# Transposes of a normalised x, a new order in the mixer's units, and GpSimd additions ahead of the products with ones

## The reference, cut to what matters

```python
y = xf * lax.rsqrt(jnp.mean(xf * xf, axis=-1, keepdims=True) + EPS)      # of x, then times g
...
s = jnp.einsum('bclhd,bcmhd->bchlm', q, k) * jnp.exp(log_d - m_row[..., None])
num = jnp.einsum('bchlm,bcmhe->bclhe', s, v) + ...
den = jnp.sum(s, axis=-1) + ...
h = num / jnp.maximum(jnp.abs(den), jnp.exp(-m_row))
...
xs = jax.vmap(lambda ub, ib: ub[ib])(u, idx)                             # the rows of each expert
```

## Time and profile before

| | us |
|---|---|
| median of 3 runs | 2302.24 |
| lowest and highest | 2298.16, 2304.51 |
| profiled execution, its time | 2301.57 |
| its span in the trace | 2299.4 |
| TensorE busy | 2134.0 (93%) |
| VectorE busy | 716.3 (31%) |
| ScalarE busy | 647.1 (28%) |
| GpSimd busy | 33.2 (1%) |
| DMA, mean rate | 315 GB/s |

### The profile page before, as it was taken

How to read it: one execution, slowest core, us unless ns; L and a number is a source line. 1 busy time by engine, 2 the same in 40 slices (tenths; PEclk the granted TensorE clock), 3 DMA queues, 4 the chain that set the end, 5 groups by cost and what they waited for, 6 DMA issues and landing times.

```text
span 2299.4 us, 27379 instructions
## 1 busy us (share of the span) xinstructions
PE 2134.0 (93%) x12059; PEld 1317.9 (57%) x12059; DVE 716.3 (31%) x1033; ACT 647.1 (28%) x1022; POOL 33.2 (1%) x54
## 2 busy tenths in 40 slices
PE   8999999889888988988988988989999999989999
PEld 8877444324323333333432432337888998978997
DVE  7756200100110010010010010016665554865653
ACT  6545200101001001001000010005465444865442
POOL 2100000000000000000000000000000000000000
PEclk9999999999999999999999999999999999999999
DMA  7435999999999999999999999997444655544653
GB/s 226 141 90 217 415 424 422 424 424 421 425 424 421 425 425 421 425 425 421 424 425 421 423 424 419 425 422 231 132 147 147 203 190 197 179 148 130 198 191 113
DMA packets 179807, 724.66 MB, mean 315 GB/s; under 512 B 11598, under 2 KB 109314, under 8 KB 130538
## 3 DMA queue, kind: packets, MB, share of 16 engines
q1 hardware_dynamic: 178472, 720.86, 79.4%
q0 software_dynamic: 640, 1.43, 0.2%
q10 hardware_dynamic: 578, 0.64, 0.1%
HBM read 721.82 MB, written 1.07 MB: 314 GB/s over the span
## 4 chain that ended last, share of the span: by engine, by line
PE 62%; DMA 30%; ACT 4%; DVE 3%; issue 1%; DVEq 0%; SPq 0%; ACTq 0%
PE bank L1250 21%; DMA weight_ring<-in_w_up_dram 17%; PE bank L1208 13%; DMA weight_ring<-in_w_gate_dram 12%; PE bank L1134 7%; PE bank L1109 5%; PE bank L777 3%; PE bank L1080 2%; PE bank L1279 1%; PE bank L1186 1%; PE bank L972 1%; PE bank L895 1%; ACT weights_ring L1981 1%; ACT squares L1916 1%; PE bank L1444 1%
## 5 line engine op out<-in xcount | busy, mean ns | idle before, releaser
L1134 PE MATMUL bank<-weight_ring,arena 128*64 128x506 f32 x3048 | 657.4, 573 | 130.3 <-DMA weight_ring<-in_w_up_dram 86.5
L1134 PEld LDWEIGHTS bank<-weight_ring,arena 128*64 128x64 f32 x3048 | 219.3, 137 | 570.1 <-issue 322.8
L1208 PE MATMUL bank<-weight_ring,arena 128*64 128x512 f32 x1408 | 305.7, 593 | 0.0
L2664 DVE TENSOR_TENSOR weights_ring<-weight_ring,weights_ring 128x2048 fp32r<-128x2048 f32 x110 | 249.6, 2289 | 147.5 <-ACT weights_ring L1981 147.3
L2632 DVE SCALAR_TENSOR_TENSOR arena<-arena,bank 128x506 f32<-128x506 f32 (+1 forms) x48 | 28.0, 638 | 822.5 <-ACT arena L1884 822.5
L1250 PE MATMUL bank<-input_high,weights_ring 128*128 128x256 f32 x1920 | 248.1, 281 | 0.0
L1250 PEld LDWEIGHTS bank<-input_high,weights_ring 128*128 128x128 f32 x1920 | 234.3, 188 | 2.7 <-issue 2.5
L1981 ACT ACTIVATE weights_ring<-weight_ring 128x2048 fp32r<-128x2048 f32 x110 | 207.4, 1908 | 62.1 <-DMA weight_ring<-in_w_ffn_down_dram 41.0
L1208 PEld LDWEIGHTS bank<-weight_ring,arena 128*64 128x64 f32 x1408 | 99.2, 137 | 195.0 <-issue 194.9
L1878 ACT ACTIVATE arena<-bank 128x512 f32<-128x512 f32 x16 | 9.6, 597 | 512.0 <-PE bank L1109 512.0
L1250 PE MATMUL bank<-input_low,weights_ring 128*128 128x256 f32 x960 | 132.1, 279 | 0.0
(11 more groups left out here) (388 smaller groups left out, 2003.9 us busy)
## 6 DMA issues: line engine op xcount, KB each, us to landing
weight_ring<-in_w_gate_dram SPq DMA_DIRECT2D x128, 1408.0 KB, 16.2
weight_ring<-in_w_down_dram SPq DMA_DIRECT2D x127, 1408.0 KB, 24.4
weight_ring<-in_w_up_dram SPq DMA_DIRECT2D x126, 1408.0 KB, 24.1
weight_ring<-in_w_ffn_gu_dram SPq DMA_DIRECT2D x44, 1024.0 KB, 5.1
weight_ring<-in_w_ffn_down_dram SPq DMA_DIRECT2D x22, 1024.0 KB, 4.8
weight_ring<-in_w_in_dram SPq DMA_DIRECT2D x16, 1024.0 KB, 5.7
arena<-in_w_xkv_dram SPq DMA_DIRECT2D x8, 2048.0 KB, 25.2
weight_ring<-in_ab_w_in_dram SPq DMA_DIRECT2D x12, 1024.0 KB, 6.1
```

The lines of the kernel that those rows point to most:

```text
L1134: last = pe.matmul(bank[first_bank + c][MPAD * half:MPAD * half + MPAD, 0:(hi - lo) * HF], xs3[:, s, :], w[:, lo:hi, HF * half:HF * half + ...
L1208: last = pe.matmul(bank[6][MPAD * half:MPAD * half + MPAD, :], hidT[:, at:at + MPAD], W[:, j * D + 512 * half:j * D + 512 * half + 512], s ...
L2664: dve.tensor_tensor(low_slot(k), raw_slot(k), high_slot(k), ALU.subtract).then_inc(S("weights_low"), 1)
```

## The change

- Start: ScalarE squares tiles 0 and 2, VectorE tile 1. The diagonal goes; VectorE scales each tile of x by its rate into `xnorm` (over the same space of the decay tables), and TensorE transposes it against the identity. TensorE's order is: tile 0, the first two of tile 1, the small vectors, the first two of tile 2, then the other six pairs.
- Units: GpSimd adds, after the probabilities of unit n, the parts of the key tiles that overlap into `key_sum` (two additions), and TensorE's products with ones run over that sum and what is left: two products over 128 and 144 columns in a forward unit, three over 128, 144 and 128 in a backward one. The values' product goes first; the ones wait for GpSimd. The semaphore `decay_ready` becomes `pool_mixer` and counts on.
- VectorE's product of unit n - 1 moves ahead of the arguments of unit n + 1; ScalarE's `hm_rates` moves ahead of the take of the projection.
- The retention scores of head 1: the wait for the last unit's product moves from the first of three products to the third.
- Token sums: VectorE adds square 7 too, and one group of sums is left, behind the router's products.
- First gather: copy, transposes and copy run in two halves (banks 7 and 5); TensorE waits for the second half ahead of weight slot 2.

```diff
@@ -197,8 +197,7 @@
 vrow = QKP[:, 0:256]
-x_squares = DEC[:, 0:D]
-rate_diag = tiles(DEC[:, D:D + TT * P], TT)
+xnorm = tiles(DEC[:, 0:TT * D], TT)
 mix_high_a = rounded("mixer_high_a", "weight_ring", CSLOTS * CSLOT, 7 * T)
@@ -465,6 +464,12 @@
 STREAM_BANKS = [4, 0, 1, 2]
+key_sum = rows[0]
+def unit_sum_ready(n):
+    return H * TT + 2 * n + 2
 MLSTM_C = 0.25 * float(P) ** -0.5
@@ -506,7 +511,7 @@
         if k == 15:
-            sp.wait_ge(S("decay_ready"), H * TT)
+            sp.wait_ge(S("pool_mixer"), H * TT)
             sp.wait_ge(S("rot_out"), 2 * H)
@@ -688,7 +693,20 @@
         blk = dec[0:ROWS[i], h, i, P * i:P * i + ROWS[i]]
-        pool.tensor_tensor(blk, blk, ident[0:ROWS[i], 0:ROWS[i]], ALU.add).then_inc(S("decay_ready"), 1)
+        pool.tensor_tensor(blk, blk, ident[0:ROWS[i], 0:ROWS[i]], ALU.add).then_inc(S("pool_mixer"), 1)
+    for n in range(8):
+        pt = tiles(SQ[:, (n % 2) * 816:(n % 2 + 1) * 816], TT)
+        lo, hi = (P, T) if n % 2 == 0 else (0, P)
+        pool.wait_ge(S("m_probs"), n + 1)
+        if n:
+            pool.wait_ge(S("num_ready"), n)
+        pool.tensor_tensor(key_sum[:, lo:hi], pt[:, 0, lo:hi], pt[:, 1, lo:hi], ALU.add).then_inc(S("pool_mixer"), 1)
+        pool.wait_ge(S("pool_mixer"), unit_sum_ready(n) - 1)
+        if n % 2 == 0:
+            lo = 2 * P
+        part = key_sum[0:ROWS[2], lo:hi]
+        pool.tensor_tensor(part, part, pt[0:ROWS[2], 2, lo:hi], ALU.add).then_inc(S("pool_mixer"), 1)
@@ -721,22 +739,27 @@
     pe.wait_ge(S("ident_landed"), 16)
-    xt3 = tiles(xtok, TT)
...
-        return pe.matmul(bank[i][:, P * j:P * j + ROWS[j]], xt3[0:ROWS[j], j, P * i:P * i + P],
-                         rate_diag[0:ROWS[j], j, 0:ROWS[j]], start=True, stop=True)
-    pe.wait_ge(S("x_rate"), 1)
+        return pe.transpose(bank[i][:, P * j:P * j + ROWS[j]], xnorm[0:ROWS[j], j, P * i:P * i + P],
+                            ident[0:ROWS[j], 0:ROWS[j]])
+    pe.wait_ge(S("ident_landed"), 16)
+    pe.wait_ge(S("x_steps"), 2)
     for i in range(KT):
         turn_x(i, 0)
+    pe.wait_ge(S("x_steps"), 3)
+    turn_x(0, 1)
+    turn_x(1, 1)
     pe.wait_ge(S("vec_landed"), 16 * sum(len(g) for g in VEC_ROWS))
...
     last.then_inc(S("vec_ready"), 1)
-    pe.wait_ge(S("x_rate"), 3)
-    for i in range(KT):
+    pe.wait_ge(S("x_steps"), 4)
+    turn_x(0, 2).then_inc(S("xt_ready"), 1)
+    turn_x(1, 2).then_inc(S("xt_ready"), 1)
+    for i in range(2, KT):
         if i == KT - 1:
@@ -888,12 +911,18 @@
         order = list(range(TT)) if d == 0 else list(range(TT))[::-1]
-        for dst, v in ((2, mv3), (3, None)):
-            for j in order:
-                lo, hi = span(d, j)
-                w = v[0:ROWS[j], j, P * h:P * h + P] if v is not None else ones[0:ROWS[j], :]
-                last = pe.matmul(bank[dst][:, lo:hi], w, pt[0:ROWS[j], j, lo:hi],
-                                 start=(j == order[0]), stop=(j == order[-1]))
+        for j in order:
+            lo, hi = span(d, j)
+            pe.matmul(bank[2][:, lo:hi], mv3[0:ROWS[j], j, P * h:P * h + P], pt[0:ROWS[j], j, lo:hi],
+                      start=(j == order[0]), stop=(j == order[-1]))
+        pe.wait_ge(S("pool_mixer"), unit_sum_ready(n))
+        if d == 0:
+            pe.matmul(bank[3][:, 0:P], ones[:], pt[:, 0, 0:P], start=True, stop=True)
+            last = pe.matmul(bank[3][:, P:T], ones[:], key_sum[:, P:T], start=True, stop=True)
+        else:
+            pe.matmul(bank[3][:, 0:P], ones[:], key_sum[:, 0:P], start=True, stop=True)
+            pe.matmul(bank[3][:, P:T], ones[0:ROWS[2], :], pt[0:ROWS[2], 2, P:T], start=True, stop=False)
+            last = pe.matmul(bank[3][:, P:2 * P], ones[:], pt[:, 1, P:2 * P], start=False, stop=True)
         last.then_inc(S("num_ready"), 1)
@@ -910,10 +939,12 @@
             pe.wait_ge(S("proj_taken_act"), 32)
-            pe.wait_ge(S("unit_out"), 8)
         else:
...
         for j in range(TT):
+            if h == 1 and j == 2:
+                pe.wait_ge(S("unit_out"), 8)
             last = pe.matmul(bank[4 * (1 - h % 2) + j][0:ROWS[j], 0:T], rk3[:, h, P * j:P * j + ROWS[j]], rq3[:, h, :],
@@ -998,13 +1029,12 @@
-    def token_sums(i):
-        sq = SQ[:, T * i:T * i + T]
+    def token_sums():
         for j in range(TT):
-            last = pe.matmul(bank[7][0:ROWS[j], j:j + 1], sq[:, P * j:P * j + ROWS[j]], ones[:, 0:1],
-                             start=(i == 0 and j == 0), stop=(i == KT - 1), skip_group_check=True)
+            last = pe.matmul(bank[7][0:ROWS[j], j:j + 1], SQ[:, P * j:P * j + ROWS[j]], ones[:, 0:1],
+                             start=(j == 0), stop=True, skip_group_check=True)
         return last
@@ -1015,12 +1045,10 @@
             router(n - 2)
-    pe.wait_ge(S("squares_added"), KT - 2)
-    token_sums(0)
     router(KT - 2)
     router(KT - 1).then_inc(S("router_ready"), 1)
-    pe.wait_ge(S("norm_squares"), KT)
-    token_sums(KT - 1).then_inc(S("norm_sum"), 1)
+    pe.wait_ge(S("squares_added"), KT - 1)
+    token_sums().then_inc(S("norm_sum"), 1)
     pe.wait_ge(S("logits_taken"), 1)
@@ -1121,6 +1149,8 @@
                 scatter(e, s // 4)
+            if use == 1 and s == 2 and e == 0:
+                pe.wait_ge(S("xs_taken"), 2)
             n = s - (ESLOTS - AHEAD)
@@ -1156,12 +1186,16 @@
     gather_first()
-    pe.wait_ge(S("rows_taken"), 1)
-    rows_to_features()
+    for b in range(2):
+        pe.wait_ge(S("rows_taken"), b + 1)
+        for i in range(2):
+            last = pe.transpose(bank[7 - 2 * b][:, P * i:P * i + P], xs_tok[:, P * (2 * b + i):P * (2 * b + i) + P], ident[:])
+        last.then_inc(S("xs_ready"), 1)
     pe.wait_ge(S("utok_taken"), 14)
...
     for e in range(EXP):
-        pe.wait_ge(S("xs_taken"), e + 1)
+        pe.wait_ge(S("xs_taken"), e + 2 if e else 1)
         hidden(e, 0, "gate_used", 1)
@@ -1188,7 +1222,7 @@
         if e + 1 < EXP:
-            pe.wait_ge(S("rows_taken"), e + 2)
+            pe.wait_ge(S("rows_taken"), e + 3)
             if e:
@@ -1211,7 +1245,7 @@
         if e == 0:
-            pe.wait_ge(S("xs_taken"), 2)
+            pe.wait_ge(S("xs_taken"), 3)
             pe.wait_ge(S("norm_out"), 8 * 2)
@@ -1629,17 +1663,24 @@
     act.wait_ge(S("tokens_landed"), 32)
-    after(act.activation(SQ[:, 0:D], tiles(xtok, TT)[:, 0, :], ACT.Square, scale=1.0 / 32, accum_out=stat[:, 0:1]))
-    for j in range(TT):
+    xt = tiles(xtok, TT)
+    def x_square(j):
         r = ROWS[j]
-        if j:
-            act.wait_ge(S("x_sums"), j)
-        else:
-            act.wait_ge(S("ident_landed"), 16)
-        rate = stat[0:r, 3 + j:4 + j]
-        after(act.activation(rate, stat[0:r, j:j + 1], ACT.Ln, bias=eps[0:r]))
-        after(act.activation(rate, rate, ACT.Exp, scale=-0.5))
-        act.activation(rate_diag[0:r, j, 0:r], ident[0:r, 0:r], ACT.Copy, scale=rate).then_inc(S("x_rate"), 1)
+        after(act.activation(SQ[0:r, 0:D], xt[0:r, j, :], ACT.Square, scale=1.0 / 32, accum_out=stat[0:r, j:j + 1]))
+    def x_rate(j):
+        rate = stat[0:ROWS[j], 3 + j:4 + j]
+        after(act.activation(rate, stat[0:ROWS[j], j:j + 1], ACT.Ln, bias=eps[0:ROWS[j]]))
+        act.activation(rate, rate, ACT.Exp, scale=-0.5).then_inc(S("x_rate"), 1)
+    x_square(0)
+    x_rate(0)
+    act.wait_ge(S("x_landed"), 32)
+    x_square(2)
+    act.wait_ge(S("x_steps"), 1)
+    x_rate(1)
+    x_rate(2)
     cast_a_to(1)
@@ -1733,7 +1774,7 @@
     values(rv, 1, TT)
-    act.wait_ge(S("decay_ready"), H * TT)
+    act.wait_ge(S("pool_mixer"), H * TT)
@@ -1760,6 +1801,8 @@
             unit_reciprocal(n - 1)
+        if n >= 4 and d == 0:
+            hm_rates(h - 2)
         k = 24 + n
@@ -1771,8 +1814,6 @@
             unit_exps(n + 1)
-        if n >= 4 and d == 0:
-            hm_rates(h - 2)
         cast_a_to(14 + n // 2)
@@ -1864,8 +1905,14 @@
-    take_rows(1)
-    take_xs(1)
+    act.wait_ge(S("rows_ready"), 1)
+    for b in range(2):
+        act.activation(xs_tok[:, 256 * b:256 * b + 256], bank[6][:, 256 * b:256 * b + 256], ACT.Copy).then_inc(S("rows_taken"), 1)
+    x4 = xs.rearrange("p (h i s) -> p h i s", h=2, s=MPAD)
+    for b in range(2):
+        act.wait_ge(S("xs_ready"), b + 1)
+        act.activation(x4[:, :, 2 * b:2 * b + 2, :], bank[7 - 2 * b][:, 0:256].rearrange("p (i h s) -> p h i s", h=2, s=MPAD),
+                       ACT.Copy).then_inc(S("xs_taken"), 1)
@@ -1901,7 +1948,7 @@
         if e + 1 < EXP:
-            take_xs(e + 2)
+            take_xs(e + 3)
         act.wait_ge(S("down_used"), 8 * e + 8)
@@ -2287,12 +2334,13 @@
     dve.wait_ge(S("x_landed"), 32)
-    for j in range(1, TT):
-        r = ROWS[j]
-        ins = dve.scalar_tensor_tensor(out=x_squares[0:r], in0=xt[0:r, j, :], scalar=1.0 / D, in1=xt[0:r, j, :],
-                                       op0=ALU.mult, op1=ALU.mult, accum_out=stat[0:r, j:j + 1])
-        ins.then_inc(S("x_sums"), 1)
-        dve.wait_ge(S("x_sums"), j)
```

(15 more changed lines are left out.)

## The result

The median after is 2285.51 us (2280.72 to 2286.99, six runs), against 2298.34 of six runs before on the same chips. The ratio is 0.9936 (0.9922 to 0.9950), which is 14.7 us less (11.5 to 17.9). The profiled execution took 2286.80 us with a span of 2285.0, so 14.4 less than the span of before. The measured time lies at the very edge of its range (2285.5), and the terms came out at other sizes than forecast.

What follows compares the result with a forecast made beforehand. Experts' weight DMA bounds 382 to 1580 us, TensorE and VectorE 28.6 to 59; savings ahead of 201 us pass fully. 2301.57 - 4.5 (start) - 6.8 (units) - 1.0 (token sums, gather) = 2289.3 us; range 2285.5 to 2298.

Steps and rivals of the forecast that it cites:

- That the gains pass to the end: Whole kernel: time saved ahead of 201 us moves the weight stream and all behind it, one for one.
- a, start: Start: scaling x on VectorE and transposing ends the first projection chunk earlier; -4.5 us, from -3.3 to -4.8.
- the last six pairs take 6 x 0.35 us: Start: the last six transpose pairs, each priced as three transposes' time, end near 15.5 us, not 21.07.
- Rival 2: Start gives half or less, TensorE at half clock until 24 us or longer: -2.3 us, time 2291.5; chance 0.12.
- b, units: Mixer units: fewer columns, stops and clock falls gone; -6.8 us, from -3.5, or 0 with late GpSimd, to -7.2.
- Fewer columns: Units' ones products: 1.5 us saved in four forward units, 0.3 in four backward ones, sum 1.8.
- Stops: Units: TensorE's two 0.5 us stops for VectorE's product go, -1.0, and one for ScalarE's rate, -0.8.
- Clock: Units: both falls to half clock go with the stops, 1.6 us each, -3.2 us; 0 if neither goes.
- c and d: Token sums -0.65 and first gather -0.7, together 1.35 us ahead of the experts; -1.0 at the end, from 0.
- 1, the clock falls at another place: Units: the clock still falls twice, at another place; time 2292.5 us; chance 0.2.
- 3: VectorE absorbs the start's gain and units gain only by fewer columns; time 2298.8 us; chance 0.1.
- 4: Units: VectorE's two-input operations hold up GpSimd's adds, 2.74 us each, in every unit; 33 us lost, 2322.6; chance 0.04.

Runs made afterwards that it cites:

- warm_start: Kernel after plus 34 products of constants on TensorE ahead of the first transpose; median 2286.31 us, ratio 0.9943 to the kernel before.
- no_sums: Kernel after with the GpSimd sums undone, so the ones products run over all their columns; ratio 0.9958 to the kernel before.
- order_only: Kernel before with the reordering alone: VectorE's product and ScalarE's rate ahead, wait of head 1's retention scores later; ratio 0.9985.
- sums_only: Kernel before with the GpSimd sums alone, VectorE's product and ScalarE's rate in their old places; ratio 0.9989.
- before_again: Kernel before, unchanged, profiled once more in a single execution; units 52.11 us, first chunk ends at 32.46 us.
- start_only: Kernel before with the start's change alone: x scaled on VectorE, transposes in place of products with the diagonal; ratio 0.9981.
- tail_only: Kernel before with one group of token sums and the first gather in halves alone; ratio 0.9987.
- pool_slow: Kernel after with four more GpSimd additions in each unit; ratio 1.0032 to the kernel before.
- pool_two: Kernel after with two more GpSimd additions in each unit; ratio 0.9960 to the kernel before.

## Why the prediction was right or wrong

**That the gains pass to the end**: right. 13.1 us at the first load, 14.4 at the experts, 14.1 at the start of the last expert's down projection, 14.4 at the end of the span.

**a, start** (-4.5 forecast; -3.46 in the pair of profiles, -3.9 on average). Much came as written: VectorE's second split starts at 19.80 (19.7 forecast), the products run slow until 20.97 (20.8 forecast), VectorE did not cap it. The step that failed is "the last six pairs take 6 x 0.35 us". A pair took 0.62, which is the distance of their rows (13.86, 14.48, 15.10), and the slow clock is most of that: in warm_start, where it was full for them, the same 14 transposes took 2.80 us instead of 4.04; I had priced them at full clock while taking half clock for the products right behind them. So TensorE came to the first chunk at 17.25, not 15.5, and none of its 48 products was done beside ScalarE's casts, where I had eight; 16 were slow, as I had it, and 32 fast where I had 24. The end is 25.16 instead of 23.9. Rival 2's mechanism, at half its size (1.0 us lost to it, where rival 2 had 2.2).

**b, units** (-6.8 forecast; -9.68). Three terms:
- Fewer columns: **-1.8 forecast, -4.5 measured** (no_sums against after). This is the term of the sum that failed, too small by 2.7 us, and by it the time came out at the edge of the range. The step is "In a backward unit the count stays and I take 0.07 x 4 = 0.3, since the weight loads, not the columns, pace these". 256 fewer columns saved 0.42 us a unit (3.00 us in no_sums, 2.58 in after), 1.6 ns a column. In a forward unit it was 0.55, not 0.38, and 0.2 more on the product that follows (3.21 to 3.00 us behind unit 0). So the columns count, whatever the weight loads do: the backward units gave 1.7 us where I had 0.3, the forward ones 3.0 where I had 1.5, less 0.2 of short stops. I had divided one row's total by twelve, where the row held products of 16 to 272 columns.
- Stops: -1.8 forecast (1.0 and 0.8), -2.0 measured by order_only. Right, though incomplete: with the sums in and the moves out they would have been 3.7 us (1.9 and 1.8 in sums_only). The two parts were costed side by side, and they depend on each other.
- Clock: -3.2 forecast, and -3.3 in the pair of profiles (55.38 against the 52.11 of before_again). The size per fall was right, and its place in the sum was not: before_again, start_only and tail_only have the stops and no fall. Of nine executions with stops of 0.5 us or more in the units, five had no half clock there, and the five without a stop had none; so few do not show that the stops bring the falls. The longest ones differ: each of the four stops of 2.0 to 3.3 us (pool_slow, pool_two) had half clock within 1 us behind it. What belongs in a forecast is a share of the 3.2, about 1 us: three falls of 1.6 in five executions, the four with the old units (2, 0, 0, 0) and sums_only (1).

So the sum came out nearer than its terms: part a fell short by 1.0 and part b was too small by 2.9. Without the luck of the clock part b is 6.4 us (52.1 to 45.7), and the forecast without it had 3.6.

**c and d** (-1.35, of which -1.0 at the end): 0.64 and 0.65 at the experts, as forecast to 0.1; what of it reaches the end is open. A fall of the clock at the gather was not in the forecast and is as large as the gain.

**Rivals.** 1, the clock falls at another place: not in the units; at the gather, in most executions of the new kernels, yes. 3 was excluded by start_only. 4 had the price right (2.74 us; 2.4 to 2.9 in the pool kernels) and VectorE's two-input operations as the cause; only the 128x2048 subtraction was seen to cost so much, and it comes near the additions of units 3, 5 and 7 alone, so "in every unit" could not come. In the kernel after none was held. The Trainium skill (GPSIMD Engine Reference, Specifications) has GpSimd contend with VectorE operations of two SBUF inputs, and the runs agree: 2.4 to 2.9 us beside the subtraction of weights, at most 0.65 in after.

## What to carry to other kernels

Price a removed instruction by the row of its own shape, never by a line's mean, and where the clock is low carry that through every step of the stretch. A shorter product on the critical engine is worth its full time only if what it waits for next is moved with it: of 4.5 us, the sums alone kept 2.4. And before a stretch of half clock in one profile enters a sum, look at a second profile of the same kernel.

## What the runs showed of the hardware

- The slow start of TensorE is not all in the record of the granted clock. In after and in before_again the view gives 1.00 from the start, yet 128x272 products take nearly twice their time, seven in 1.79 us instead of 1.04. The length of equal products is the surer sign.
- Where the full clock comes varies between executions of one program: 24 us in one profile of before, and between 27.8 and 29.2 in the other, by the length of its products. The Trainium skill (TensorE: Matmul & The Clock Gate, The HAM clock gate) says that the moment varies from run to run; here it was most of the 3.84 us between the two ends of the first chunk.
- A GpSimd addition that meets VectorE's 128x2048 subtraction can be held until that has ended: additions that started from 0.29 us ahead of it to 0.48 us behind its start ended 0.3 us after its end (0.6 in the earlier trace rows). One that started 0.26 us ahead took 0.65 us, and there the subtraction took 2.54 instead of 2.27.
- Six stops of 0.4 to 3.3 us in pool_slow, 12.0 us in all, came with the clock at half for 15.7 of the units' 66 us, so that a stop cost 1.7 times its length.
- From the start of the last expert's down projection to the end it took 748 to 758 us, in executions of kernels that do not differ there; such scatter hides changes of 1 or 2 us.
